# The first modulation blocks of a two-block transformer kernel: summed on TensorE in 16 transfers instead of on VectorE in 4

## The reference, cut to what matters

```python
c_act = jax.nn.silu(c)                                       # (1, 1024)
for i in range(2):
    mod = (c_act @ mod_w[i] + mod_b[i]).reshape(B, 3, 3, D)  # mod_w[i]: (1024, 9216)
    shift, scale, gate = mod[:, :, 0], mod[:, :, 1], mod[:, :, 2]
    h = rms_norm(x, norm_g[i, 0]) * (1.0 + scale[:, 0]) + shift[:, 0]
    x = x + 0.5 * gate[:, 0] * swiglu(h, w_gate, w_up, w_down)
    ...                                                      # attention, then a second swiglu, in the same way
```

## Time and profile before

| | us |
|---|---|
| median of 3 executions | 2005.62 |
| lowest and highest | 2004.48, 2010.59 |
| the profiled execution, whole | 2009.78 |
| its span, first to last instruction | 2008.0 |
| TensorE busy in the span | 1894.2 (94%) |
| VectorE busy | 1421.8 (71%) |
| ScalarE busy | 941.4 (47%) |
| mean granted TensorE clock | 0.958 |
| share of TensorE in the chain that ended last | 87% |

### The profile page before, as it was taken

The page is one execution under the profiler, slowest core; times in us unless marked ns, Lnnn a source line. Parts: engine busy times, 40 slices in busy tenths (PEclk is TensorE's granted clock), DMA queues, the critical chain, the costliest instruction groups (busy, mean ns, idle before and its releaser), DMA issues.

```text
span 2008.0 us, 32297 instructions
## 1 busy us (share of the span) xinstructions
PE 1894.2 (94%) x11974; PEld 1696.1 (84%) x11974; DVE 1421.8 (71%) x2103; ACT 941.4 (47%) x1357; POOL 303.9 (15%) x292
## 2 busy tenths in 40 slices
PE   2999999899999999999999999999889998989998
PEld 2998777799989998888878799877779986769997
DVE  6777888677777777667755655556579956657994
ACT  2444465444444443455454544454564445545443
POOL 1001010000110010000000000009712102941210
PEclk8999999899999999899999999998799998889999
DMA  9778776357787776354520454552155554114553
GB/s 364 263 279 278 259 241 201 125 201 270 284 288 256 272 281 224 140 188 169 187 105 1 165 186 174 191 199 99 63 171 188 182 195 140 71 61 158 180 187 126
DMA packets 61412, 382.12 MB, mean 190 GB/s; under 512 B 6896, under 2 KB 6896, under 8 KB 24448
## 3 DMA queue, kind: packets, MB, share of 16 engines
q1 hardware_dynamic: 41040, 300.96, 42.1%
q0 software_dynamic: 19856, 77.93, 11.5%
q10 hardware_dynamic: 432, 2.08, 0.3%
HBM read 379.89 MB, written 1.05 MB: 190 GB/s over the span
## 4 chain that ended last, share of the span: by engine, by line
PE 87%; DVE 8%; ACT 2%; issue 2%; DMA 1%; SPq 0%; DVEq 0%; ACTq 0%
PE ps L496 13%; PE ps L497 13%; PE ps L498 13%; PE ps L462 11%; PE ps L464 11%; PE ps L463 11%; DVE ring_lo L1485 1%; PE ps L780 1%; PE ps L517 1%; PE ps L543 1%; PE ps L568 1%; PE ps L519 1%; PE ps L518 1%; DMA arena<-in_mod 1%; PE ps L900 1%
## 5 line engine op out<-in xcount | busy, mean ns | idle before, releaser
L1485 DVE TENSOR_TENSOR ring_lo<-ring,w_hi 128x1024 fp32r<-128x1024 f32 x534 | 657.4, 1240 | 347.1 <-ACT w_hi L1079 342.9
L1079 ACT ACTIVATE w_hi<-ring 128x1024 fp32r<-128x1024 f32 x556 | 586.6, 1059 | 634.8 <-PE ps L498 326.4
L496 PE MATMUL ps<-h_lo,w_hi 128*128 128x256 f32 x2112 | 601.9, 285 | 10.1 <-issue 6.0
L497 PE MATMUL ps<-h_hi,w_hi 128*128 128x256 f32 x2112 | 601.1, 285 | 0.0
L498 PE MATMUL ps<-h_hi,ring_lo 128*128 128x256 f32 x2112 | 601.0, 285 | 0.0
L496 PEld LDWEIGHTS ps<-h_lo,w_hi 128*128 128x128 f32 x2112 | 409.2, 194 | 11.9 <-issue 7.3
L497 PEld LDWEIGHTS ps<-h_hi,w_hi 128*128 128x128 f32 x2112 | 409.1, 194 | 0.0
L498 PEld LDWEIGHTS ps<-h_hi,ring_lo 128*128 128x128 f32 x2112 | 409.0, 194 | 0.0
L462 PE MATMUL ps<-w_hi,h_lo 128*128 128x512 f32 x604 | 250.7, 415 | 23.6 <-DVE h_lo L1874 6.4
L463 PE MATMUL ps<-ring_lo,h_hi 128*128 128x512 f32 x604 | 242.8, 402 | 0.0
L464 PE MATMUL ps<-w_hi,h_hi 128*128 128x512 f32 x604 | 242.5, 402 | 0.0
(11 more groups left out here) (325 smaller groups left out, 2152.1 us busy)
## 6 DMA issues: line engine op xcount, KB each, us to landing
ring<-in_stream SPq DMA_DIRECT2D x278, 1024.0 KB, 4.8
arena<-in_mod POOLq DMA_DIRECT2D x128, 512.0 KB, 5.5
arena<-in_mod SPq DMA_DIRECT2D x3, 2048.0 KB, 17.3
gate<-in_wide POOLq DMA_DIRECT2D x3, 1536.0 KB, 10.9
arena<-in_nsaw POOLq DMA_DIRECT2D x2, 1072.0 KB, 12.2
arena<-in_mod SPq DMA_DIRECT2D x1, 1536.0 KB, 26.6
arena<-in_konst POOLq DMA_DIRECT2D x1, 1295.5 KB, 9.2
arena<-in_mixw POOLq DMA_DIRECT2D x2, 576.0 KB, 12.8
```

The lines of the kernel that those rows point to most:

```text
L496: nc.tensor.matmul(dst, hi, x_lo, start=(r == 0 and i == 0 and b % 2 == 0), stop=False)
L497: nc.tensor.matmul(dst, hi, x_hi, start=False, stop=False)
L1079: nc.scalar.activation(w_hi[:, q % SPLITS, :], ring[:, half % SLOTS, (q % 2) * QUARTER:(q % 2 + 1) * QUARTER], ACT.Copy).then_inc(w_hi_rea ...
L1485: v.tensor_tensor(ring_lo[:, slot, cs], ring[:, slot, cs], w_hi[:, q % SPLITS, :], ALU.subtract).then_inc(w_lo_ready, 1)
```

## The change

SyncE's queue now carries, in this order and with no wait between them: `cols`, `konst`, `x`, sixteen transfers of 512 KB (four for each of the first four steps, each holding two chunks, each with a semaphore of its own), and the four ring slots. ScalarE starts no transfer. TensorE sums the first four steps itself: for each landed transfer and each of its two chunks, four matmuls with a 128x128 block of `mod_w` as the stationary operand and one column of `cact` as the moving one, into one column of four PSUM banks, eight in a row accumulating; 128 matmuls in all, in place of the 32 with ones. They stand behind `norm(0)` on TensorE. VectorE's 32 operations of `mod_begin` go; it reads the sums from the four banks. The rounding and subtraction of quarters 0 to 2 (`split`) move from before and after the modulated norm into it: one quarter behind each of its first three of four parts. GpSimd's first modulation load waits for the first rounded quarter (`w_hi_ready`) instead of `first_done`.

```diff
-        mod_first = [[arena[:, 0:STEP]], [arena[:, STEP:2 * STEP]], [arena[:, A0 + 2048:A0 + 2048 + STEP]],
-                     [arena[:, 2 * STEP:2 * STEP + 3072], wa[:, :]]]
+        mod_first = [arena[:, at + r * QUARTER:at + (r + 1) * QUARTER] for at in (0, STEP, A0 + 2048, 2 * STEP) for r in range(4)]
+        mod_first[-1] = wa[:, :]
...
         # SyncE
-            for q in range(FIRST):
-                at = 0
-                for part in mod_first[q]:
-                    w = min(part.shape[1], STEP - at)
-                    sp.dma_start(part[:, 0:w], a["mod"][q, :, at:at + w]).then_inc(first_in[q], 16)
-                    at += w
-            for q in range(FIRST):
-                sp.wait_ge(first_in[q], 16 * len(mod_first[q]))
+            sp.dma_start(cols[:, :], a["cols"]).then_inc(cols_in, 16)
+            sp.dma_start(konst[:, :], a["konst"]).then_inc(x_in, 16)
+            sp.dma_start(x[:, :, :], a["x"]).then_inc(x_in, 16)
+            for n in range(4 * FIRST):
+                sp.dma_start(mod_first[n], a["mod"][n // 4, :, n % 4 * QUARTER:(n % 4 + 1) * QUARTER]).then_inc(first_in[n], 16)
             for h in range(SLOTS):
                 sp.dma_start(ring[:, h, :], a["stream"][h, :, :]).then_inc(slot_full[h], 16)
...
         # GpSimd
-            pool.wait_ge(first_done, FIRST - 1)
+            pool.wait_ge(w_hi_ready, 1)
             for r in range(4):
                 mod_load(FIRST, r)
...
         # TensorE: norm(0), then in place of mod_cols(0, [0])
+            def mod_first_cols():
+
+                pe.wait_ge(cact_ready, 1)
+                for n in range(4 * FIRST):
+                    pe.wait_ge(first_in[n], 16)
+                    for i in range(2):
+                        k = n % 4 * 2 + i
+                        for b in range(4):
+                            o = i * 512 + b * P
+                            mm = nc.tensor.matmul(ps[:, b, n // 4:n // 4 + 1], mod_first[n][:, o:o + P], cact[:, k:k + 1],
+                                                  start=(k == 0), stop=(k == KC - 1))
                 mm.then_inc(col_sum, 1)
...
         # ScalarE and VectorE, norm_parts(m), behind each of the four parts b
+                    if m == 0:
+                        split(b, min(b + 1, LEAD))
...
         # ScalarE
-            act.dma_start(cols[:, :], a["cols"]).then_inc(cols_in, 16)
-            act.dma_start(x[:, :, :], a["x"]).then_inc(x_in, 16)
-            act.dma_start(konst[:, :], a["konst"]).then_inc(x_in, 16)
             act.wait_ge(cols_in, 16)
...
-            split(0, 2)
             norm_parts(0)
-            split(2, LEAD)
...
         # VectorE
-            def mod_begin(first, end):
...
+            def mod_first_cols():
+
+                dve.wait_ge(col_sum, 1)
+                b, g = COLS["mod_b"], COLS["norm_g"]
+                tick.mark(v.tensor_tensor(modcol[:, 0, :, :].rearrange("p w (h c) -> p (w h) c", h=2), ps[:, 0:4, 0:FIRST].rearrange("p c s -> p s c"),
+                                          cols[:, b:b + 16].rearrange("p (s c) -> p s c", s=FIRST), ALU.add))
+                tick.settle()
+                v.scalar_tensor_tensor(out=modcol[:, 0, 1, :], in0=modcol[:, 0, 1, :], scalar=1.0, in1=cols[:, g:g + 8],
+                                       op0=ALU.add, op1=ALU.mult).then_inc(col_ready, 1)
+                dve.wait_ge(col_ready, 1)
...
             dve.wait_ge(cact_ready, 1)
-            mod_begin(0, 3)
             dve.wait_ge(x_in, 16 * 2)
             dve.wait_ge(konst_in, 16 * 3)
             norm(0)
-            mod_begin(3, FIRST)
-            split(0, 2)
-            mod_cols(0, [0], 1)
+            mod_first_cols()
             norm_parts(0)
-            split(2, LEAD)
```

More of the change, by code:

```diff
@@ L239, in build @@
         dil_oT = xn[:, :, :].rearrange("p t (c n) -> p (t c) n", n=T)
-        mod_first = [[arena[:, 0:STEP]], [arena[:, STEP:2 * STEP]], [arena[:, A0 + 2048:A0 + 2048 + STEP]],
-                     [arena[:, 2 * STEP:2 * STEP + 3072], wa[:, :]]]
-        assert FIRST == len(mod_first)
+        mod_first = [arena[:, at + r * QUARTER:at + (r + 1) * QUARTER] for at in (0, STEP, A0 + 2048, 2 * STEP) for r in range(4)]
+        mod_first[-1] = wa[:, :]
+        assert len(mod_first) == 4 * FIRST
         a0 = 5632
@@ L287, in build @@
         cols_in, x_in, konst_in, late_in, gate_in, mix_in = [sem(n) for n in ("cols_in", "x_in", "konst_in", "late_in", "gate_in", "mix_in")]
-        first_in = [sem(f"first_in{i}") for i in range(FIRST)]
-        first_done = sem("first_done")
+        first_in = [sem(f"first_in{i}") for i in range(4 * FIRST)]
         mod_in = [sem(f"mod_in{i}") for i in range(MRING)]
@@ L556, in mod_cols @@
             def mod_cols(layer, subs, bank=0):
-                start = layer == 0 and subs == [0]
-                if not start:
-                    pe.wait_ge(mod_used, 4 * (MODQ * layer + 6 * subs[-1] + 4 - FIRST))
+                pe.wait_ge(mod_used, 4 * (MODQ * layer + 6 * subs[-1] + 4 - FIRST))
                 for s in subs:
@@ L563, in mod_cols @@
                         for c in range(KC):
-                            if start and c % 4 == 0:
-                                pe.wait_ge(first_done, 2 * kind + c // 4 + 1)
                             o = (MODQ * layer + 6 * s + 2 * kind) % ACCS * 512 + c * P
@@ L568, in mod_cols @@
                             mm = nc.tensor.matmul(ps[:, bank, at:at + 1], accs[:, o:o + P], ones[:, 0:1], start=True, stop=True)
+                mm.then_inc(col_sum, 1)
+            def mod_first_cols():
[8 more added lines that the diff above has]
+                                                  start=(k == 0), stop=(k == KC - 1))
                 mm.then_inc(col_sum, 1)
@@ L1041, in _ @@
             norm(0)
-            mod_cols(0, [0])
+            mod_first_cols()
             ffn(0, False, 0)
```

## The result

The changed kernel takes 2038.43 us (median of 4, 2036.33 to 2040.74) against 2007.36 for the kernel before (median of 4): ratio 1.0153, interval 1.0134 to 1.0171. It is 31 us slower. The prediction gave 2011.3 and a range up to 2018; it had the sign of its middle right and the size wrong by a factor of five.

The account below looks back on a forecast made before the run. It took TensorE to bound the kernel, and VectorE, then the loads, to bound the head. With tables in at N = 10.0, the first product came at 50.0 instead of 44.27, 5.7 us later: 2005.62 became 2011.3, range 2004 to 2018.

Parts of the forecast that it names:

- Step 3: Head, TensorE's 128 new one-column matmuls: 0.216 us each at 1.2 GHz, 27.8 us in all, not held up by loads.
- Step 1, N: Start of the head: N, when `x`, `konst`, `cols` and GpSimd's three tables are in, at 10.0, bounds 9.3 to 14.7.
- The rival that had GpSimd's tables still at 14.7: Start of the head: tables no sooner than before, TensorE's chain 4.7 us later, loss 10.4 us, 2016; chance 0.15.
- Step 2: Head, ScalarE, VectorE and transposes: transposes start at N + 4.1, TensorE's next work at N + 7.4.
- Steps 4 and 5: End of head: `modcol` 0.65 us after the last one-column matmul; first product 2.93 us later plus 1.2 for the moved `split`.
- Step 6: GpSimd's modulation loads, now behind the first rounded quarter: no cost, with 3.6 us to spare.
- Step 7: Start of the feed-forward: TensorE at 0.50 clock for about 4.8 us, before as after; no change, give or take 1 us.
- The last words on what follows as one block: Everything behind the first product: time after it as before, to the microsecond.
- The first (full clock held): Head matmuls: clock stays at 2.4 GHz, first product at 36.1, 8.2 us earlier, 1995 to 1997; chance 0.12.
- The second (raised once): After the transposes: clock raised once for 3.3 us, worth 3.2 us, so 2.5 us later than before, 2008; chance 0.2.
- The chance of 0.35 for slower: Whole kernel: 0.2 for the forecast's loss beyond 6 us plus 0.15 for GpSimd's tables still at 14.7.

Follow-up runs that it names:

- Experiments 1 and 2: one_pass and half_chunks, in that order, each made from the changed kernel; profiled spans 2010.6 and 2008.0 us instead of 2036.8.
- experiment 3: Also called split_back: changed kernel with rounding and subtraction of quarters 0 and 1 back ahead of `modcol`, quarter 2 behind the norm parts; ratio 1.0157 to the kernel before.
- row_moving: Changed kernel with the sums' operands exchanged: one `cact` column stationary, 512 `mod_w` columns moving, 32 matmuls, row not turned into columns; span 2014.6 us.
- one_pass: Changed kernel with the 128 matmuls on fp32r operands, two `cact` columns moving, four rounded transfers standing for all sixteen; profiled span 2010.6 us.
- half_chunks: Changed kernel summing only the first of each transfer's two chunks, 64 matmuls instead of 128; profiled span 2008.0 us.
- hybrid2: Kernel before with the new transfer order, TensorE summing one transfer in four, VectorE three, `norm(0)` behind TensorE's first transfer; ratio 0.9982 to the kernel before.
- early_shared: Kernel before with four `mod_w` transfers ahead of `konst` and `x`, VectorE summing all but one transfer of each of the first two steps, left to TensorE; ratio 0.9979.

## Why the prediction was wrong, point by point

*Step 3, the 128 new matmuls, failed.* "127 x 0.216 + 0.35 = 27.8 us" mixes a price per record with a number of instructions. The trace has 256 records in 54.6 us, 0.213 each. With that one term mended, the first product comes at 50.0 + 54.6 - 27.8 = 76.8, measured 76.49, and the prediction's own sum is 2011.3 + 54.6 - 27.8 = 2038.1; measured 2038.43. That the sum agrees to 0.3 us is in part luck, since executions of one kernel differ by some 4 us and the median before, 2005.62 in the sum, is 2007.36 with one more execution. Experiments 1 and 2 show that the two records of a float32 matmul are two passes, each at full price.

*What was right in step 3:* the pace. The one-column matmuls of the changed kernel ran at 1.2 GHz throughout, neither raising nor, in the kernels where it was raised, keeping the clock, and the loads didn't hold them up. Even at 2.4 GHz the corrected count would not have paid: 256 x 0.108 = 27.6 us from 17.3, and the 4.6 us that TensorE idles before the first product, make 49.5, still 5 us behind 44.27.

*Step 1, N:* 10.0 forecast, 9.77 measured; turns on the queues explain it well enough, though no run took the turns apart. The rival that had GpSimd's tables still at 14.7 did not happen in any run (9.7 to 10.6).

*Step 2:* the transposes at N + 4.1 forecast, 13.86 - 9.77 = 4.09 measured; the next work at N + 7.4 forecast, 7.5 measured.

*Steps 4 and 5:* 4.1 us from `modcol` to the first product forecast, 4.16 measured, 2.94 with the split moved back (experiment 3).

*Step 6:* no gap on TensorE where VectorE waits for GpSimd's later loads; right. *Step 7:* about 4.8 us at 1.2 GHz at the start of the feed-forward forecast, 4.5 measured, from 76.49 to 81.0. *The last words on what follows as one block:* behind the first product the nine experiments and the two kernels have 1960 to 1966 us left, so the shift of the first product is the change of the time, within what executions differ.

*The rivals.* The first (full clock held) did not happen. The second (raised once) is real, at 3 us, and comes in some profiles and not in others; it was given a chance of 0.2 as a case of its own, while in truth it lies on top of all the others. The chance of 0.35 for slower rested on a late N alone. None of the rivals had a price for the new matmuls above 27.8 us: I bounded the price of one from both sides and never the number.

## What to carry to other kernels

Before a price per record is multiplied by a number read in the source, count the records of one known call in the trace against that call's source: here 32 against 16 for float32 matmuls, 16 against 16 for the transposes, 24 against 24 for the fp32r products. A matrix-vector product with the matrix standing still makes TensorE load 128 columns of weights to stream one; it leaves TensorE busy, slow, and at the low clock, and VectorE with 0.78 us per 128x512 chunk beats its 8 passes of 0.213 (1.7 us). When a part of a change wins 18 us at an early point of the head, ask what the next thing in the head is limited by: here all 18 us and 32 more went into it.

## What the runs showed of the hardware that I had not expected

- A plain float32 matmul is recorded as two passes of TensorE, each with its own weight load: 256 records for 128 matmuls, and 64 for 32 with 512 columns moving. The Trainium skill (FP8 and Floating Point Precision, on true FP32) speaks of four passes. The trace shows two records; in row_moving each of them took 2 cycles a streamed column at 2.4 GHz, four cycles a column for both, which agrees with four passes if a record holds two of them. No run shows what lies within a record. In a one-column matmul it is hardly the streamed column that costs: at 1.2 GHz passes with one column, with two (one_pass) and with 256 all come 0.21 us apart. That leaves the weight loads, which is argued and not measured on its own.
- An fp32r matmul with a 128x128 stationary operand and two columns has the same pace as one float32 pass, 0.21 us at 1.2 GHz (88 records in 18.5 us in one_pass).
- Sixteen float32 transposes, 0.21 us apart, were at times followed by the full clock (half_chunks, one_pass, split_back) and at times not (the changed kernel, hybrid2, early_shared). The Trainium skill (TensorE: Matmul & The Clock Gate, on the PE-mode transpose) says that the full clock doesn't engage for transposes, which don't count as busy in the same way. split_back speaks against it: TensorE had done nothing but transposes when the clock rose, at 17.15, before the last of them; the sixteen took 3.26 us there and 3.65 in the changed kernel, and the passes behind them were at 2.4 GHz:

```profile
14.42 3.26 PE L539 MATMUL ps<-konst,xn 128*128 128x128 f32 x16 [14.42 <-DVE xn L1498]
```

```profile
17.60:21.00 3.40, 3.40 (x32) 3.40 (x31) 0.00 (x0) 0.00 (x0) 0.00 (x0) 0.94 1.03 411
```

- The clock column reads 1.00 in stretches ahead of the first change that the profile recorded, whatever the clock was. The windows of split_back show the same work at the same pace as the changed kernel from 45 to 65 (96 records in 20 us), with a recorded change before it:

```profile
40.00:60.00 20.00, 20.00 (x95) 20.00 (x96) 0.00 (x0) 0.00 (x0) 0.00 (x0) 0.50 0.45 182
```

The spacing of the records tells the clock there, the column does not.
